# Third norm's transposes under the last output-projection groups, router products by pairs of tiles, three of its four normalised tiles computed on POOL

## The reference

```python
x = x + memory_cross_attention(rms_norm(x, xattn_norm_g[l]), rms_norm(mem, mem_norm_g[l]),
                               xattn_wq[l], xattn_wk[l], xattn_wv[l], xattn_wo[l])
x = x + hier_moe(rms_norm(x, ffn_norm_g[l]), router_coarse_w[l], router_coarse_b[l],
                 router_fine_w[l], router_fine_b[l], exp_w_gate[l], exp_w_up[l], exp_w_down[l])
...
def rms_norm(x, g):
    xf = x.astype(jnp.float32)
    y = xf * lax.rsqrt(jnp.mean(xf * xf, axis=-1, keepdims=True) + EPS)
    return (y * g.astype(jnp.float32)).astype(x.dtype)
```

## Time and profile before

| what | value |
|---|---|
| timed runs | 794.27, 793.6, 794.35 us; median 794.27 |
| profiled execution | 793.41 us, span 791.5 us |
| PE, DVE, ACT, POOL busy | 95%, 67%, 58%, 23% of the span |
| chain that ended last, by engine | PE 91%, DVE 3%, ACT 3% |
| DMA engines busy while experts run | 90% or more in nearly every slice from 440 to 770 us |

### The profile page before, as it was taken

The page is one execution under the profiler, slowest core; times in us unless marked ns, Lnnn a source line. Parts: engine busy times, 40 slices in busy tenths (PEclk is TensorE's granted clock), DMA queues, the critical chain, the costliest instruction groups (busy, mean ns, idle before and its releaser), DMA issues.

```text
span 791.5 us, 11744 instructions
## 1 busy us (share of the span) xinstructions
PE 754.3 (95%) x4204; PEld 588.1 (74%) x4204; DVE 531.1 (67%) x706; ACT 458.4 (58%) x680; POOL 179.2 (23%) x185
## 2 busy tenths in 40 slices
PE   3999999999999999999999969999999999999994
PEld 3978789767788889888898854577777777777763
DVE  4535369588782546532363289589998898899986
ACT  4445663487784235532352152478787887877862
POOL 2900023000000101000000010035555544455312
PEclk9999999999999999999999999999999999999998
DMA  9833531000305424532103759999999999999962
GB/s 296 208 115 110 162 104 58 1 2 2 144 18 173 147 82 152 200 128 104 54 2 106 292 189 363 367 378 385 383 380 367 376 379 372 375 382 382 380 213 106
DMA packets 61903, 166.90 MB, mean 211 GB/s; under 512 B 8224, under 2 KB 36192, under 8 KB 49576
## 3 DMA queue, kind: packets, MB, share of 16 engines
q1 hardware_dynamic: 56376, 150.69, 51.5%
q0 software_dynamic: 4480, 12.48, 6.7%
q10 hardware_dynamic: 1008, 3.21, 1.1%
HBM read 153.44 MB, written 12.85 MB: 210 GB/s over the span
## 4 chain that ended last, share of the span: by engine, by line
PE 91%; DVE 3%; ACT 3%; issue 1%; DMA 0%; POOL 0%; POOLq 0%; ACTq 0%; DVEq 0%
PE ps L1949 23%; PE ps L1951 22%; PE ps L1950 22%; PE ps L2209 3%; PE ps L2159 2%; PE ps L2251 2%; PE ps L2398 2%; PE ps L2237 2%; PE ps L2070 2%; PE ps L2140 1%; PE ps L2137 1%; PE ps L2378 1%; PE ps L2320 1%; PE ps L2141 1%; DVE tok L1376 1%
## 5 line engine op out<-in xcount | busy, mean ns | idle before, releaser
L1356 DVE TENSOR_TENSOR wlo<-raw,whi 128x2048 fp32r<-128x2048 f32 x30 | 68.7, 2291 | 90.6 <-ACT whi L890 90.6
L1949 PE MATMUL ps<-whi,mhi 128*96 128x512 f32 (+1 forms) x276 | 109.4, 396 | 2.0 <-DVE mlo L1881 1.2
L1951 PE MATMUL ps<-whi,mlo 128*96 128x512 f32 (+1 forms) x276 | 108.8, 394 | 0.0
L1950 PE MATMUL ps<-wlo,mhi 128*96 128x512 f32 (+1 forms) x276 | 108.2, 392 | 0.0
L1364 DVE TENSOR_TENSOR wlo<-arena,whi 128x2048 fp32r<-128x2048 f32 x39 | 89.3, 2290 | 18.9 <-ACT whi L903 18.9
L746 POOL TENSOR_SCALAR stat<-stat 128x1 f32<-128x1 f32 x18 | 11.6, 642 | 364.5 <-ACT tok L909 215.2
L903 ACT ACTIVATE whi<-arena 128x2048 fp32r<-128x2048 f32 x39 | 74.7, 1916 | 24.8 <-PE ps L1951 24.8
L890 ACT ACTIVATE whi<-raw 128x2048 fp32r<-128x2048 f32 x30 | 57.3, 1911 | 54.2 <-PE ps L1951 54.1
L1949 PE MATMUL ps<-whi,ahi 128*128 128x512 f32 (+1 forms) x192 | 71.1, 370 | 4.8 <-DVE wlo L1356 4.8
L1949 PE MATMUL ps<-ahi,whi 128*128 128x512 f32 x192 | 75.6, 394 | 0.0
L1951 PE MATMUL ps<-ahi,wlo 128*128 128x512 f32 x192 | 74.8, 390 | 0.0
(11 more groups left out here) (391 smaller groups left out, 1689.4 us busy)
## 6 DMA issues: line engine op xcount, KB each, us to landing
arena<-in_exp_w_gate SPq DMA_DIRECT2D x30, 1024.0 KB, 17.4
arena<-in_exp_w_up SPq DMA_DIRECT2D x17, 1024.0 KB, 17.1
raw_a<-in_exp_w_down SPq DMA_DIRECT2D x16, 1024.0 KB, 18.4
raw<-in_exp_w_up SPq DMA_DIRECT2D x15, 1024.0 KB, 5.0
arena<-in_exp_w_down SPq DMA_DIRECT2D x9, 1024.0 KB, 25.6
raw<-in_exp_w_down SPq DMA_DIRECT2D x7, 1024.0 KB, 17.6
raw<-in_w_in SPq DMA_DIRECT2D x5, 1024.0 KB, 6.4
raw<-in_w_in SPq DMA_DIRECT2D x10, 512.0 KB, 6.9
```

The lines of the kernel that those rows point to most:

```text
L1356: v.tensor_tensor(wlo[:, n % SPLIT, :], raw[:, n % RAW, :], whi[:, n % SPLIT, :].bitcast(F32), ALU.subtract).then_inc(lo_done, 1)
L1949: mm(out_, ahi_, bhi_, start=first, stop=False)
L1950: mm(out_, ahi_, blo_, start=False, stop=False)
L1951: return mm(out_, alo_, bhi_, start=False, stop=last)
```

## The change

PE: tile 0's transposes go behind tile 1's group of `xo3` and tile 1's behind tile 2's; tile 2's go into the middle of tile 3's group, ahead of its seventh matmul. Behind the last group comes `narrow` of tiles 0 and 1, then tile 3's transposes, `to_tokens` of tiles 0 and 1, `narrow` of tiles 2 and 3 and their `to_tokens`.

DVE: `norm_last` stays for tile 0 alone; the low parts of tiles 0 and 1 go ahead of tile 3's evacuation. It waits for all of H3 ahead of the comparison at L1821, since POOL now uses `tok`.

POOL: for tiles 1 to 3 it makes the factor, then multiplies X by it into `tok`, waits, and multiplies by the gain into H3. ACT: squares and high parts alternate, and the first `router_out` stands between the last square and tile 3's high part.

```diff
@@ gpsimd
-            for q in range(NT, N4):
+            for q in range(NT, N3 + 1):
                 rms(q)
+            pool.wait_ge(gain_full, 64)
+            for t in range(1, NT):
+                rms(N3 + t)
+                if t == 1:
+                    pool.wait_ge(h_done, N3 + 1)
+                pool.wait_ge(rms_done, N3 + t + 1)
+                lanes, g = "t (q k) -> t q k", gbc[:, :]
+                pool.tensor_scalar(tok[:, t, :], X[:, t, :], stat[:, 2, N3 + t:N3 + t + 1], None, ALU.mult).then_inc(h_scaled, 1)
+                pool.wait_ge(h_scaled, t)
+                pool.tensor_tensor(H3[:, t, :].rearrange("t (k q) -> t q k", k=KD), tok[:, t, :].rearrange(lanes, k=KD),
+                                   g.rearrange(lanes, k=KD), ALU.mult).then_inc(h_done, 1)
@@ scalar
-            for t in range(3):
-                square_last(t)
-            for t in range(NT):
-                norm_hi(N3 + t, ahi, t)
+            square_last(0)
+            square_last(1)
+            norm_hi(N3, ahi, 0)
+            norm_hi(N3 + 1, ahi, 1)
+            square_last(2)
+            norm_hi(N3 + 2, ahi, 2)
+            square_last(3)
             router_out(0)
-            square_last(3)
+            norm_hi(N3 + 3, ahi, 3)
             router_out(1)
@@ vector
             evacuate(ND - 1, (2,))
-            norm_last(1)
             norm_lo(N3, alo, ahi, 0)
+            norm_lo(N3 + 1, alo, ahi, 1)
             evacuate(ND - 1, (3,))
-            for t in range(1, NT):
-                norm_lo(N3 + t, alo, ahi, t)
-            norm_last(2)
+            norm_lo(N3 + 2, alo, ahi, 2)
+            norm_lo(N3 + 3, alo, ahi, 3)
...
-            dve.wait_ge(logits_done, 1)
+            dve.wait_ge(logits_done, 2)
             dve.wait_ge(rms_done, N4)
...
-            norm_last(3)
...
+            dve.wait_ge(h_done, N4)
@@ tensor
                         for k in range(KF):
                             kk = KF * c0 + k
+                            if (ORDER[n], idx, k) == ("xo3", NT - 1, KF // 2):
+                                norm_transposes(N3 + 2, X[:, 2, :])
...
-                        if (ORDER[n], idx) == ("xo3", 2):
-                            norm_transposes(N3, X[:, 0, :])
+                        if ORDER[n] == "xo3" and 0 < idx < NT - 1:
+                            norm_transposes(N3 + idx - 1, X[:, idx - 1, :])
...
-            for t in range(1, NT):
-                norm_transposes(N3 + t, X[:, t, :])
...
+            pair_logits(0)
+            norm_transposes(N3 + 3, X[:, 3, :])
+            pair_tokens(0)
+            pair_logits(1)
+            pair_tokens(1)
```

More of the change, by code:

```diff
@@ L492, in build @@
         h_done = sem("h_done")
+        h_scaled = sem("h_scaled")
         ntp_done = sem("ntp_done")
@@ L2292, in _, with pair_logits, pair_tokens @@
                 dense(n)
-            for t in range(1, NT):
-                norm_transposes(N3 + t, X[:, t, :])
             pe.wait_ge(sm_lo, 2)
-            pe.wait_ge(evac["dve"], evacs(len(groups) - 1, "dve"))
-            for b in range(2):
+            def pair_logits(b):
+                pe.wait_ge(evac["dve"], evacs(of_piece[ND - 1][b], "dve"))
                 pe.wait_ge(ntp_lo, 2 * (N3 + 2 * b + 2))
                 narrow(ps[b], wrt2, ROUT_W, 2 * P * b, 2 * P).then_inc(route_mm, 1)
-            for b in range(2):
+            def pair_tokens(b):
                 pe.wait_ge(rT_done, b + 1)
-                ins = to_tokens(ps[2], rT, fold_r, ROUT_W, range(2 * b, 2 * b + 2))
-            ins.then_inc(logits_done, 1)
+                to_tokens(ps[2], rT, fold_r, ROUT_W, range(2 * b, 2 * b + 2)).then_inc(logits_done, 1)
+            pair_logits(0)
[3 more added lines that the diff above has]
+            pair_tokens(1)
             pe.wait_ge(onehot_done, 1)
```

## The result

The changed kernel takes **797.8 us** (median of 6 runs, 797.06 to 798.9) against 794.15 us for the kernel before, in 6 runs on the same chip (793.11 to 794.35). The two medians lie 0.46% apart; the ratio estimated from all the runs is 1.0054 (95% interval 1.0044 to 1.0064). That is slower, well clear of no change. The profiled execution took 797.06 us, its span 795.2 us.

The account below looks back on a forecast made before the run. PE bounds the kernel, so a delay at the first pick reaches the end whole. 1.02 us (tile 3's later transposes) plus 0.1 (POOL holding the router chain) made 1.1, on 794.27 giving 795.4 us; range 793.9 to 798.0.

Parts of the forecast that it names:

- Rival 1: DVE's router chain: POOL's multiplications hold it, deciding from X = 3.5 on; 798.6 us at X = 4.6; chance 0.30.
- X: POOL's time for both multiplications of one tile: taken as 3.5 us (1.43 and 2.10), between 2.0 and 4.6.
- Transposes under the groups: PE's projection groups: new sets for tiles 1 and 2, 0.90 us each, end tile 3's group 1.8 us later.
- No wait of PE for tile 2's set: Inside tile 3's group, PE reaches tile 2's transposes at 459.4, inputs ready: costs nothing, cover a tenth of a microsecond.
- rivals 3 and 4: 3: clock falls early around the second product, 797.3, chance 0.06; 4: PE waits in tile 3's group, 796.7, chance 0.06.
- The order behind the group: Behind PE's last group, the first pair's product precedes tile 3's transposes: these and the logits come 1.02 us later.
- POOL's multiplications: POOL's norms of tiles 1 to 3: with X = 3.5 the last multiplication ends at 469.9, between 465.3 and 473.1.
- 459.3 + 3X: Formula for when POOL's last multiplication ends, three tiles at X each: 469.9 with X = 3.5.
- Why that end matters: DVE's router chain: its second operation, at 469.8, waits for POOL's end at 469.9, costing 0.1 us.
- 3 us for each microsecond of X: Cost of POOL holding the router chain for X above 3.5; 3.3 us at X = 4.6.
- The late factor: On POOL, tile 3's factor behind two tiles of multiplications becomes the wait for the logits if POOL ends later still; unsized.
- The rest costs nothing: Behind the picks and in SP's writes: the lists' inputs, H3 writes and weights hold nobody, cost nothing.

Follow-up runs that it names:

- e1: The changed kernel without POOL's two full-width multiplications for tiles 1 to 3, other engines' order kept: 794.54 us, 1.0011 of the kernel before.
- e5: The changed kernel without POOL's multiplications, tile 3's high part before the first router copy; PE does tile 3's transposes, both products, then both turns: 794.37 us.
- e9: The changed kernel with POOL multiplying by the gain first, then making factors 2 and 3, then scaling tiles 2 and 3: 796.26 us, 1.0040 of before.
- e6: The changed kernel with only tile 1's norm on POOL, tile 2's transposes behind the last group, then tile 3's, both products, both turns: 792.47 us.

## Why the prediction was wrong

The forecast of 795.4 was 2.4 us short, and slower had the smaller chance. Rival 1 happened: the term for POOL's hold on the chain, 0.1 us in the sum, measured 3.3. That the range (793.9 to 798.0) held the time is luck: its upper end goes with X up to 4.4, and X was 5.2; too high a price for each microsecond of X made up for that. By its steps:

- *Transposes under the groups*: right. Tile 3's evacuation stands at t0+10.82; from 461.95 in the text, t0+10.88 was forecast.
- *No wait of PE for tile 2's set; rivals 3 and 4*: right to cost nothing. No idle PE inside tile 3's group, and the clock fell only behind the logits.
- *The order behind the group*: right. Tile 3's transposes at t0+12.49 (forecast 12.53), an idle of 1.12 us ahead of the second product (forecast 1.4), 0.93 for the path as counted above and 0.87 in e1 (forecast 1.02). The experiments put it down to what was forecast: e5, with both products side by side again, is back to 0.38 behind the kernel before.
- *POOL's multiplications*: **this step failed.** X was 5.2 to 5.3 (5.24 on average), above my upper end of 4.6, and not 3.5. The formula 459.3 + 3X held: with 5.24 it gives 475.0 against t0 of before, 474.0 with the change's earlier t0, and the trace has 474.23. The multiplication by the gain was near my choice (2.10; it took 2.35 to 2.42). The scaling was the error: from a memset I took 1.43 and at most 1.86, and it took 2.85, more than the operation with two inputs; three times that difference of 1.42 is 4.3 of the 5.2 us by which POOL ended later than reckoned. My upper end charged the input at the rate at which a memset writes, 0.86 for 1024 columns; no row showed that rate for a read, so it was no bound. What makes the scaling slow no run shows.
- *Why that end matters*: right in kind, wrong in form. I counted one wait up to POOL's end, at the chain's second operation. In fact the scaling held that operation for 0.69 and the multiplication a later one for 2.09, with eight operations at their old lengths between. "3 us for each microsecond of X" was too much: POOL let part of the chain through. At X = 5.24 it gives 5.2 us for the late end; all of POOL's effect was 3.3, the late factor included. That the text has 3.3 for X = 4.6 too is chance. Of the two rows behind this step, the cast of the earlier trace rows was read too closely: it ended at 118.85, 0.27 us behind the memsets (118.58), and no row has it alone.
- *The late factor*: named in rival 1 but not priced; 0.53.
- *The rest costs nothing*: the lists' inputs (488.51) were ready ahead of PE (491.14), as forecast. Not in it was the clock: the stretch at half clock lasted 3.4 us longer, which cost the picks 0.44. The wait of 1.2 us in the earlier trace rows was misplaced: it stands at 766.9, behind the expert loop; where the loop begins PE waits 0.8, and in the change 0.7. Nothing in the sum rested on it.

The Trainium skill (SBUF — State Buffer, Who interferes with whom) says the port pair that POOL and DVE share is locked by whichever operation comes first, for the whole of it. The multiplication by the gain agrees (DVE released 0.08 us behind its end); the scaling does not, as the trace shows the chain's operations released 1.2 us into 2.85, with the one in the step ahead of the chain (L1741) against that.

## What to carry to other kernels

Work moved to POOL was not off DVE's path here while it ran beside a chain of short DVE operations with two SBUF inputs: end it before that chain begins, or leave it on DVE where DVE has room. A small step that others wait for, such as a factor, must not be queued behind long ones on the same engine. On PE, put work that depends on nothing new into the waits that are there (tile 2's transposes under tile 3's evacuation) and keep turns that wait for another engine's copy behind the last product.

## What was not expected of the hardware

- POOL's scaling of 128x1024 by a column took 2.85 to 2.87 us, longer than its multiplication of two 128x1024 inputs with a lane-wise write, 2.35 to 2.42. Why was not tried.
- Its hold on the router chain lasted 1.20 to 1.24 us from its start, in the four cases seen. Eight DVE operations, five of them with two SBUF inputs, ran at their old lengths in what was left of it in the change. The one-input step at L1741, held to the end of another scaling, is the exception.
- The hold works the other way too. In e9 POOL's first multiplication began 0.23 us into DVE's norm and took 4.02 us instead of 2.4, in e6 a factor's step took 1.80 instead of 0.19 beside tile 2's norm. First the timeline of e9, then that of e6:

```profile
454.50 2.12 DVE L1403 SCALAR_TENSOR_TENSOR arena<-arena,stat,gbc 128x1024 f32<-128x1024 f32 x1
...
454.73 4.02 POOL L808 TENSOR_TENSOR tok<-arena,gbc 128x1024 f32<-128x1024 f32 x1 [0.65 <-DVE arena L1513]
```

```profile
463.85 2.06 DVE L1391 SCALAR_TENSOR_TENSOR arena<-arena,stat,gbc 128x1024 f32<-128x1024 f32 x1
464.03 1.80 POOL L747 TENSOR_SCALAR stat<-stat 128x1 f32<-128x1 f32 x1 [1.16 <-ACT arena L921]
```
